# Summing eight expert rows per token: halves of the eight rows, or halves of the row

## The chip, the cores and the metric

One Trainium2 chip, one core of it. The metric is the device time of one execution in microseconds (us); less is better. All times of lines and windows come from one profiled execution, counted from the start of its span.

## The reference, cut to what matters

The program is a small diffusion backbone: two layers over 256 latent tokens (and, in layer 0, 256 context tokens beside them), width 1024. Each layer is a token mixer followed by a mixture of experts in which each token goes to 8 of 64 experts. What the change touches is the last step of a layer: for each token the eight rows that its experts wrote are summed, the sum is scaled by the gate `g2` and added to the residual stream, and the stream is normalised for what comes next (the first norm of layer 1, or the final norm).

```python
def rms_norm(x, g):
    y = xf * lax.rsqrt(jnp.mean(xf * xf, axis=-1, keepdims=True) + RMS_EPS)
    return (y * g.astype(jnp.float32)).astype(x.dtype)
...
        routed = jnp.zeros((T + 1, D), f32).at[tok_buf].add(y.reshape(P, D))[:T]
...
        h = modulate(rms_norm(x, norm1_g[i]), sh1, sc1)
...
        x = x + g2 * f[:B * S].reshape(B, S, D)
    return rms_norm(x, final_g)
```

All of it is fp32. The expert rows are already multiplied by their routing weights, and the shared expert was added to the stream earlier, so the step here is a plain sum of eight rows.

## The kernel before

The kernel is one program of phases, each a block in which all five engines have their own instruction list and which ends with all of them meeting. Within a phase the engines are ordered by semaphores only; nothing of the next phase starts before the last one is over. The phase that the change touches is `combine_phase` (L1747 on), which runs twice: in layer 0 over 4 tiles of 128 tokens, in layer 1 over 2 tiles. In the second run it is also the end of the program.

The experts have scattered their rows to the DRAM tensor `y_rows`, so that the eight rows of a token (TOPK = 8, 1024 floats, 4 KB each) lie one behind the other. A tile is 128 tokens on 128 partitions, and its 4 MB are loaded in two parts of 2 MB into four buffers of `c_rows`. Part 0 is the first four rows of each token, part 1 the last four; on either side a partition's piece is 16 KB in one run.

* SyncE (L1778 to L1781) issues the loads in order, tile by tile, part 0 then part 1; after the first two it issues the loads of the next modulation rows (two of 1 MB, layer 0) or of the final gain (0.5 MB, layer 1). A load of tile t from t = 2 on waits until the tile two before is out of its buffer: part 0 on TensorE (`pe_summed`), part 1 on VectorE (`summed`).
* TensorE (L1795 to L1803) sums part 0: four rows times two halves of 512 columns, each a matmul with the identity that accumulates in PSUM.
* VectorE (L1813 to L1829) sums part 1 with an add over 2048 elements a partition (L1816) and one over 1024 (L1818), then adds TensorE's sum from PSUM (L1821), multiplies by the gate (L1823) and adds to the stream `x_stream` (L1825), 1024 elements a partition each.
* ScalarE (L1807 to L1809) takes the row's sum of squares (L325) and the root (L327) when the stream's tile is complete.
* VectorE finishes the norm (L332, L334 and, in layer 0 alone, L340). It does so one tile late: after tile t's adds it does the norm of tile t-1, and the last tile's norm follows behind the loop.

In layer 1 the two tiles of `h` are then stored to the output (L1789).

Of the kernel before, what the change touches and what calls it, by code (L numbers as in the profile page):

```python
# [25 lines left out]
ALU = mybir.AluOpType  # L26
ACT = mybir.ActivationFunctionType
AX = mybir.AxisListType

P = 128  # L30
D = 1024
# [31 lines left out]
TOPK = 8  # L63
# [1683 lines left out]
def combine_phase(g, layer, tiles):  # L1747


    nc = g.nc  # L1750
    tag = f"c{layer}"
    H = D // 2
    KH = TOPK // 2
    jobs = [(t, part) for t in range(tiles) for part in range(2)]
    with ExitStack() as st:
        sb = lambda n, s, d=F32: st.enter_context(nc.sbuf_tensor(f"{tag}_{n}", s, d))
        rows = sb("rows", [P, 4, KH, D])
        total = sb("total", [P, 2, D])
        rows_in = [g.sem(f"{tag}_rows_in{q}") for q in range(4)]
        summed, pe_summed, scaled = g.sem(f"{tag}_summed"), g.sem(f"{tag}_pe_summed"), g.sem(f"{tag}_scaled")  # L1760
        halved, merged = g.sem(f"{tag}_halved"), g.sem(f"{tag}_merged")
        src = g.y_rows[0:tiles * P * TOPK, :].rearrange("(t p k) d -> t p k d", p=P, k=TOPK)
        added, mod_in, stored = g.sem(f"{tag}_added"), g.sem(f"{tag}_mod_in"), g.sem(f"{tag}_stored")
        gate2 = [g.mod(t, GATE2) for t in range(tiles)]
        if layer == 0:
            g.mod_layer = 1
            norm = NormRows(g, "n3", lambda t: g.mod(t, SH1), lambda t: g.mod(t, SC1))
        else:
            gain = sb("gain", [P, D])
            norm = NormRows(g, "nf", None, lambda t: gain[:])  # L1770
        with nc.Block() as block:
            @block.sync
            def _(sp):
                def load_mods():
                    for dst, stream, a, b in MOD_LOADS1[0:2]:
                        sp.dma_start(g.mod_slots(dst, b - a), g.mod_source(1, stream, a, b)).then_inc(mod_in, 16)

                for n, (t, part) in enumerate(jobs):  # L1778
                    if n >= 4:
                        sp.wait_ge(pe_summed if part == 0 else summed, t - 1)  # L1780
                    sp.dma_start(rows[:, n % 4, :, :], src[t][:, part * KH:(part + 1) * KH, :]).then_inc(rows_in[n % 4], 16)  # L1781
                    if n == 1 and layer == 0:
                        load_mods()
                    if n == 1 and layer == 1:
                        sp.dma_start(gain[:], g.ins["final_g"].partition_broadcast(P)).then_inc(mod_in, 16)  # L1785
                if layer == 1:
                    for t in range(tiles):
                        sp.wait_ge(norm.ready, t + 1)
                        sp.dma_start(g.out[0, t * P:(t + 1) * P, :], g.h[:, t, :]).then_inc(stored, 16)  # L1789
                    sp.wait_ge(stored, 16 * tiles)  # L1790

            @block.tensor
            def _(pe):

                for t in range(tiles):  # L1795
                    pe.wait_ge(rows_in[2 * (t % 2)], 16 * (t // 2 + 1))
                    if t >= 2:
                        pe.wait_ge(merged, t - 1)
                    for k in range(KH):
                        for n in range(2):  # L1800
                            last = pe.matmul(g.ps[:, 2 * (t % 2) + n, :], g.ident, rows[:, 2 * (t % 2), k, n * H:(n + 1) * H],  # L1801
                                             start=(k == 0), stop=(k == KH - 1))
                    last.then_inc(pe_summed, 1)  # L1803

            @block.scalar
            def _(act):
                for t in range(tiles):  # L1807
                    act.wait_ge(added, t + 1)
                    norm.act(act, t)  # L1809

            @block.vector
            def _(dve):
                for t in range(tiles):  # L1813
                    b, sums = 2 * (t % 2) + 1, total[:, t % 2, :]
                    dve.wait_ge(rows_in[b], 16 * (t // 2 + 1))
                    dve.tensor_tensor(rows[:, b, 0:2, :], rows[:, b, 0:2, :], rows[:, b, 2:4, :], ALU.add).then_inc(halved, 1)  # L1816
                    dve.wait_ge(halved, t + 1)
                    dve.tensor_tensor(sums, rows[:, b, 0, :], rows[:, b, 1, :], ALU.add).then_inc(summed, 1)  # L1818
                    dve.wait_ge(summed, t + 1)
                    dve.wait_ge(pe_summed, t + 1)  # L1820
                    dve.tensor_tensor(sums, g.ps[:, 2 * (t % 2):2 * (t % 2) + 2, :].rearrange("p a b -> p (a b)"), sums, ALU.add).then_inc(merged, 1)  # L1821
                    dve.wait_ge(merged, t + 1)
                    dve.tensor_tensor(sums, sums, gate2[t], ALU.mult).then_inc(scaled, 1)  # L1823
                    dve.wait_ge(scaled, t + 1)
                    dve.tensor_tensor(g.x[:, t, :], g.x[:, t, :], sums, ALU.add).then_inc(added, 1)  # L1825
                    if t:
                        dve.wait_ge(mod_in, 32 if layer == 0 else 16)
                        norm.dve(dve, t - 1)
                norm.dve(dve, tiles - 1)  # L1829


# [401 lines left out]
def backbone(nc, ins, table, out):  # L2233
    with ExitStack() as stack:
# [16 lines left out]
        with ExitStack() as layer:  # L2251
            g.mods_rest = layer.enter_context(nc.sbuf_tensor("mods_rest", [P, 4, D], F32))
            ada_phase(g)
            turned = ExitStack()
            with ExitStack() as att:
                sb = lambda n, s, d=F32: att.enter_context(nc.sbuf_tensor(n, s, d))
                qT = sb("qT", [P, HEADS // 2, TOK])
                kT = sb("kT", [P, KV // 2, 2, TOK])
                v = sb("v", [P, TILES, KVD])
                qkv_phase(g, qT, kT, v)  # L2260
                o = sb("o", [P, TILES, QD])
                attention_phase(g, qT, kT, v, o)
                g.turned_rows(turned, "hT0", TILES)
                project_phase(g, "ao", ins["attn_w_o"][0].rearrange("(p k) n -> p k n", k=KD), P, KD, TILES, src=o, spare=(qT, kT, v))
            with ExitStack() as moe:
                sb = lambda n, s, d=F32: moe.enter_context(nc.sbuf_tensor(n, s, d))
                routes, weights = Routes(sb, 0, TILES), ExpertWeights(g, sb, 0)
                route_phase(g, 0, TILES, routes, weights)
                turned.close()
                expert_phase(g, 0, TILES, routes, weights)  # L2270
            combine_phase(g, 0, TILES)
        g.recycle_semaphores()

        with ExitStack() as layer:
            turned = ExitStack()
            with ExitStack() as lru:
                sb = lambda n, s, d=F32: lru.enter_context(nc.sbuf_tensor(n, s, d))
                hsum = sb("hsum", [RP, RB, SEQ])
                with ExitStack() as inner:
                    sb = lambda n, s, d=F32: inner.enter_context(nc.sbuf_tensor(n, s, d))  # L2280
                    par = sb("par", [RW, 11 * RB])
                    uc = sb("uc", [RP, RB, TOK])
                    gate = sb("gate", [P, LAT_TILES, RNN])
                    lru_in_phase(g, par, uc, gate, hsum)
                    lru_scan_phase(g, par, uc, gate, hsum)
                g.turned_rows(turned, "hT1", LAT_TILES)
                project_phase(g, "lo", ins["lru_w_out"][0].rearrange("(n c) d -> c n d", c=RW), RW, RB, LAT_TILES, srcT=hsum)
            with ExitStack() as moe:
                sb = lambda n, s, d=F32: moe.enter_context(nc.sbuf_tensor(n, s, d))
                routes, weights = Routes(sb, 1, LAT_TILES), PairWeights(g, sb, 1)  # L2290
                route_phase(g, 1, LAT_TILES, routes, weights)
                turned.close()
                expert_pair_phase(g, 1, LAT_TILES, routes, weights)
            combine_phase(g, 1, LAT_TILES)
# [70 lines left out]
```

## Time and profile before

| what | value |
|---|---|
| median of 3 runs | 2297.92 us (2296.35 to 2297.92) |
| the profiled execution's own time | 2296.35 us |
| its span, first to last instruction | 2294.5 us |
| busy: TensorE matmul, VectorE, ScalarE | 83%, 49%, 34% of the span |
| the combine phase of layer 0 | from 1203.1 to 1263.1 us |
| the combine phase of layer 1 | from 2257.4 to the span's end |
| the two together | some 97 us, 4% of the span |

The profile's shares are averages over phases with different limits, and for this change they say little: the busiest engine of the whole, TensorE, is not what sets the length of the combine phase. That has to be read from the timeline of the two stretches, engine by engine.

### The profile page before, as it was taken

What the parts mean: (1) busy time and instruction counts of PE and PEld (TensorE: products, weight loads), DVE (VectorE), ACT (ScalarE), POOL (GpSimd) and SP (SyncE); (2) the same over time, 40 slices, a digit from 0 to 9 for tenths busy, and PEclk for the clock granted to TensorE, in tenths of its full rate; (3) what the DMA queues carried; (4) which work ended last, traced back from release to release, by engine and by line L of the source; (5) the groups of instructions that cost most, each with busy time, mean ns of one, the idle gap of its engine ahead of it and who ended that gap; (6) DMA issues with size and microseconds to landing.
All of it is one profiled execution on the core that took longest, in us unless ns stands there. A gap on an engine that the chain in (4) does not pass through costs nothing. (4 is left out here: it accounts for less than half of the span.)

```text
span 2294.5 us, 33559 instructions
## 1 busy us (share of the span) xinstructions
PE 1910.6 (83%) x9971; PEld 1297.1 (57%) x9972; DVE 1132.9 (49%) x2243; ACT 791.6 (34%) x1283; POOL 318.2 (14%) x333
## 2 busy tenths in 40 slices
PE   2889997889999999999986886637778788888884
PEld 0778844467777777777762881103445455555552
DVE  2325622577777777777756555893132121121123
ACT  1214411145555555555531456870101111111111
POOL 0220010011111111121110102221001111111110
PEclk9999997989999999999997997768889999999997
DMA  6850054158998899999957416304439999999994
GB/s 242 288 201 2 1 227 166 45 211 322 345 340 328 331 333 347 346 340 336 339 179 325 132 54 199 118 17 129 187 136 420 412 383 404 399 414 392 412 408 199
DMA packets 128294, 597.07 MB, mean 260 GB/s; under 512 B 32633, under 2 KB 51129, under 8 KB 67441
## 3 DMA queue, kind: packets, MB, share of 16 engines
q1 hardware_dynamic: 92512, 509.97, 58.5%
q0 software_dynamic: 35584, 84.31, 9.8%
q10 hardware_dynamic: 144, 2.10, 0.2%
q8 instruction: 31, 0.51, 0.1%
q14 instruction: 23, 0.18, 0.0%
HBM read 596.17 MB, written 56.20 MB: 284 GB/s over the span
## 5 line engine op out<-in xcount | busy, mean ns | idle before, releaser
L1459 DVE TENSOR_TENSOR m_w_lo<-m_wgu,m_w_hi 128x1024 fp32r<-128x1024 f32 x264 | 314.9, 1222 | 159.9 <-ACT m_w_hi L1383 145.8
L1383 ACT ACTIVATE m_w_hi<-m_wgu 128x1024 fp32r<-128x1024 f32 x264 | 269.7, 1053 | 196.0 <-DMA m_wgu<-in_moe_w_up 133.1
L1630 PE MATMUL ps<-m_wgu,m_xT 128*64 128x256 f32 x2112 | 262.2, 404 | 75.5 <-DMA m_wgu<-in_moe_w_up 58.6
L1630 PEld LDWEIGHTS ps<-m_wgu,m_xT 128*64 128x64 f32 x2112 | 186.3, 146 | 162.5 <-issue 118.8
L1325 PE MATMUL ps<-m_wd,m_hidT 128*128 128x512 f32 x528 | 237.6, 593 | 0.3 <-ACT m_hidT L1407 0.3
L1340 PE MATMUL ps<-m_w_hi,m_x_hi 128*128 128x512 f32 x528 | 213.2, 404 | 6.7 <-DVE m_x_lo L1451 6.3
L1340 PE MATMUL ps<-m_w_lo,m_x_hi 128*128 128x512 f32 x528 | 208.5, 395 | 0.0
L1340 PE MATMUL ps<-m_w_hi,m_x_lo 128*128 128x512 f32 x528 | 207.8, 394 | 0.0
L1725 DVE SCALAR_TENSOR_TENSOR m_hid<-m_act_g,m_meta,ps 128x256 f32<-128x256 f32 x33 | 15.9, 481 | 335.3 <-ACT m_act_g L1679 335.3
L1325 PEld LDWEIGHTS ps<-m_wd,m_hidT 128*128 128x128 f32 x528 | 95.3, 190 | 95.1 <-issue 95.1
L1266 POOL DMA_INDIRECT y_rows<-h,m_sidx x66 | 67.6, 1024 | 554.4 <-DVE h L1467 554.4
L1657 PE MATMUL ps<-m_wd,m_hidT 128*64 128x512 f32 x528 | 123.8, 610 | 21.9 <-ACT m_hidT L1682 14.7
L1679 ACT ACTIVATE m_act_g<-ps 128x256 f32<-128x256 f32 x33 | 12.7, 384 | 313.0 <-PE ps L1630 313.0
L1340 PEld LDWEIGHTS ps<-m_w_hi,m_x_hi 128*128 128x128 f32 x528 | 100.5, 190 | 26.5 <-issue 7.1
L1340 PEld LDWEIGHTS ps<-m_w_lo,m_x_hi 128*128 128x128 f32 x528 | 100.3, 190 | 21.5
L1340 PEld LDWEIGHTS ps<-m_w_hi,m_x_lo 128*128 128x128 f32 x528 | 100.5, 190 | 19.2
L325 ACT ACTIVATE squares<-x_stream 128x1024 bf16<-128x1024 f32 x16 | 16.9, 1053 | 261.8 <-DVE x_stream L864 140.7
L1657 PEld LDWEIGHTS ps<-m_wd,m_hidT 128*64 128x64 f32 x528 | 42.5, 139 | 80.5 <-issue 80.5
L1575 POOL DMA_INDIRECT h<-h_rows,m_gidx x35 | 35.6, 1017 | 376.4 <-DVE m_gidx L1713 370.2
L1451 DVE TENSOR_TENSOR m_x_lo<-ps,m_x_hi 128x512 fp32r<-128x512 f32 x134 | 85.9, 683 | 0.5 <-ACT m_x_hi L1373 0.5
L1801 PE MATMUL ps<-c_rows,table 128*128 128x512 f32 x96 | 51.5, 698 | 41.4 <-DMA c_rows<-y_rows 41.4
L1390 ACT ACTIVATE h<-ps 128x512 f32<-128x512 f32 x66 | 39.4, 597 | 130.2 <-PE ps L1325 130.2
(317 smaller groups left out, 3438.5 us busy)
## 6 DMA issues: line engine op xcount, KB each, us to landing
m_wgu<-in_moe_w_gate SPq DMA_DIRECT2D x132, 1024.0 KB
m_wgu<-in_moe_w_up SPq DMA_DIRECT2D x132, 1024.0 KB
m_wd<-in_moe_w_down SPq DMA_DIRECT2D x132, 1024.0 KB, 9.7
c_rows<-y_rows SPq DMA_DIRECT2D x12, 2048.0 KB, 14.9
mods<-in_ada_w POOLq DMA_DIRECT2D x11, 1024.0 KB, 6.6
mods<-in_ada_w SPq DMA_DIRECT2D x11, 1024.0 KB, 4.9
mods<-in_lru_w_in SPq DMA_DIRECT2D x7, 1280.0 KB, 6.9
ada_w<-in_ada_w SPq DMA_DIRECT2D x8, 1024.0 KB, 17.8
```

Source lines behind the costliest of these rows:

```text
L325: act.activation(g.junk[:], g.x[:, t, :], ACT.Square, accum_out=g.sumsq[:, t:t + 1]).then_inc(self.squared, 1)
L1266: pool.indirect_dma_start(g.y_rows[0:tiles * P * TOPK, :], bass.IndirectOffsetOnAxis(ap=sidx[q][:, 0:1], axis=0), ysb[q], None, bounds_che ...
L1325: last = pe.matmul(g.ps[0:S, YB + n, :], hidT[:, j, :], wd[:, q, j, n * 512:(n + 1) * 512], start=(j == 0), stop=(j == KF - 1))
L1340: last = pe.matmul(g.ps[0:S, GU, :].rearrange("p (a f) -> p a f", a=2), x[:, q, k, :], w[:, :, k, :], start=(k == 0 and n == 0), stop=(k = ...
L1383: act.activation(w_hi[:, :, k, :], wgu[:, q, :, k, :], ACT.Copy).then_inc(hi_s, 1)
L1390: act.activation(ysb[q][:, 0:512], g.ps[0:S, YB, :], ACT.Copy).then_inc(y_a, 1)
L1451: dve.tensor_tensor(x_lo[:, q, ks, :], g.ps[:, XB + n, 0:4 * S].rearrange("p (k c) -> p k c", c=S), x_hi[:, q, ks, :].bitcast(F32), ALU.su ...
L1459: dve.tensor_tensor(w_lo[:, :, k, :], wgu[:, q, :, k, :], w_hi[:, :, k, :].bitcast(F32), ALU.subtract).then_inc(lo_s, 1)
L1575: pool.indirect_dma_start(xg, None, g.h2_rows[0:tiles * P, :], bass.IndirectOffsetOnAxis(ap=gidx[:, 0:1], axis=0), bounds_check=last_token ...
L1630: last = pe.matmul(g.ps[half[s], GU, a * FE:(a + 1) * FE], xT[:, k, half[s]], wgu[:, s, a, k, :], start=(k == 0), stop=(k == KD - 1))
L1657: last = pe.matmul(g.ps[half[s], YB + n, :], hidT[:, j, half[s]], wd[:, s, j, n * 512:(n + 1) * 512], start=(j == 0), stop=(j == KF - 1))
L1801: last = pe.matmul(g.ps[:, 2 * (t % 2) + n, :], g.ident, rows[:, 2 * (t % 2), k, n * H:(n + 1) * H], start=(k == 0), stop=(k == KH - 1))
```

## The change

The two parts of a tile are cut the other way. Part h is now half h of the columns (512 of 1024) of all eight rows, so a partition's 16 KB come as eight pieces of 2 KB, 4 KB apart in DRAM. TensorE sums the eight rows of the left half (h = 0) in one PSUM bank, VectorE those of the right half (h = 1), with one `tensor_reduce` over the eight rows in place of two adds. The reduce reads `rows` as "p d k", so its innermost step is from one row to the next, 512 floats or 2 KB apart. The two halves need no merging: the gate multiply and the add to the stream are done per half, on 512 elements, first for h = 1, then for h = 0, whose multiply reads PSUM. The norm of tile t now follows at once behind tile t's adds instead of one tile later. The semaphores `halved` and `merged` go.

```diff
-    KH = TOPK // 2
-    jobs = [(t, part) for t in range(tiles) for part in range(2)]
+    jobs = [(t, h) for t in range(tiles) for h in range(2)]
...
-        rows = sb("rows", [P, 4, KH, D])
-        total = sb("total", [P, 2, D])
+        rows = sb("rows", [P, 4, TOPK, H])
+        total = sb("total", [P, 2, H])
...
-                    sp.dma_start(rows[:, n % 4, :, :], src[t][:, part * KH:(part + 1) * KH, :]).then_inc(rows_in[n % 4], 16)
+                    sp.dma_start(rows[:, n % 4, :, :], src[t][:, :, h * H:(h + 1) * H]).then_inc(rows_in[n % 4], 16)
...
-                        pe.wait_ge(merged, t - 1)
-                    for k in range(KH):
-                        for n in range(2):
-                            last = pe.matmul(g.ps[:, 2 * (t % 2) + n, :], g.ident, rows[:, 2 * (t % 2), k, n * H:(n + 1) * H],
-                                             start=(k == 0), stop=(k == KH - 1))
+                        pe.wait_ge(scaled, 2 * (t - 1))
+                    for k in range(TOPK):
+                        last = pe.matmul(g.ps[:, t % 2, :], g.ident, rows[:, 2 * (t % 2), k, :], start=(k == 0), stop=(k == TOPK - 1))
...
-                    act.wait_ge(added, t + 1)
+                    act.wait_ge(added, 2 * (t + 1))
...
-                for t in range(tiles):
-                    b, sums = 2 * (t % 2) + 1, total[:, t % 2, :]
-                    dve.wait_ge(rows_in[b], 16 * (t // 2 + 1))
-                    dve.tensor_tensor(rows[:, b, 0:2, :], rows[:, b, 0:2, :], rows[:, b, 2:4, :], ALU.add).then_inc(halved, 1)
-                    dve.wait_ge(halved, t + 1)
-                    dve.tensor_tensor(sums, rows[:, b, 0, :], rows[:, b, 1, :], ALU.add).then_inc(summed, 1)
-                    dve.wait_ge(summed, t + 1)
-                    dve.wait_ge(pe_summed, t + 1)
-                    dve.tensor_tensor(sums, g.ps[:, 2 * (t % 2):2 * (t % 2) + 2, :].rearrange("p a b -> p (a b)"), sums, ALU.add).then_inc(merged, 1)
-                    dve.wait_ge(merged, t + 1)
-                    dve.tensor_tensor(sums, sums, gate2[t], ALU.mult).then_inc(scaled, 1)
-                    dve.wait_ge(scaled, t + 1)
-                    dve.tensor_tensor(g.x[:, t, :], g.x[:, t, :], sums, ALU.add).then_inc(added, 1)
-                    if t:
+                for n, (t, h) in enumerate((t, h) for t in range(tiles) for h in (1, 0)):
+                    q = n % 2
+                    x = g.x[:, t, h * H:(h + 1) * H]
+                    gate = gate2[t][:, h * H:(h + 1) * H]
+                    if h == 0:
+                        dve.wait_ge(pe_summed, t + 1)
+                        sums = g.ps[:, t % 2, :]
+                    else:
+                        b = 2 * (t % 2) + 1
+                        dve.wait_ge(rows_in[b], 16 * (t // 2 + 1))
+                        sums = total[:, q, :]
+                        dve.tensor_reduce(sums, rows[:, b, :, :].rearrange("p k d -> p d k"), AX.X, ALU.add).then_inc(summed, 1)
+                        dve.wait_ge(summed, t + 1)
+                    dve.tensor_tensor(total[:, q, :], sums, gate, ALU.mult).then_inc(scaled, 1)
+                    dve.wait_ge(scaled, n + 1)
+                    dve.tensor_tensor(x, x, total[:, q, :], ALU.add).then_inc(added, 1)
+                    if h == 0 and t + 1 < tiles:
+
                         dve.wait_ge(mod_in, 32 if layer == 0 else 16)
-                        norm.dve(dve, t - 1)
+                        norm.dve(dve, t)
                 norm.dve(dve, tiles - 1)
```

## Rows read from the trace of the kernel before

**Rows 1.** The timeline, layer 0: start us, us, engine, line, operation, tiles [idle before, releaser].

```profile
1203.10 0.81 SPq L1781 DMA_DIRECT2D c_rows<-y_rows  x2
...
1215.19 2.29 DVE L1816 TENSOR_TENSOR c_rows<-c_rows 128x2048 f32<-128x2048 f32 x1 [17.65 <-DMA c_rows<-y_rows]
...
1222.55 1.23 DVE L1825 TENSOR_TENSOR x_stream<-x_stream,c_total 128x1024 f32<-128x1024 f32 x1
...
1229.94 2.29 DVE L1816 TENSOR_TENSOR c_rows<-c_rows 128x2048 f32<-128x2048 f32 x1 [6.16 <-DMA c_rows<-y_rows]
...
1240.55 2.29 DVE L1816 TENSOR_TENSOR c_rows<-c_rows 128x2048 f32<-128x2048 f32 x1
...
1244.63 8.83 PE L1801 MATMUL ps<-c_rows,table 128*128 128x512 f32 x16 [2.65 <-DMA c_rows<-y_rows]
...
1250.44 2.28 DVE L1816 TENSOR_TENSOR c_rows<-c_rows 128x2048 f32<-128x2048 f32 x1
...
1260.33 0.16 DVE L332 RECIPROCAL rstd<-root 128x1 f32<-128x1 f32 x1
...
1261.84 1.22 DVE L340 TENSOR_TENSOR h<-h,mods 128x1024 f32<-128x1024 f32 x1
```

**Rows 2.** The timeline, layer 1, same columns.

```profile
2269.68 2.29 DVE L1816 TENSOR_TENSOR c_rows<-c_rows 128x2048 f32<-128x2048 f32 x1 [21.81 <-DMA c_rows<-y_rows]
...
2279.57 1.28 ACT L327 ACT_TABLE_LOAD   x1
...
2281.13 2.29 DVE L1816 TENSOR_TENSOR c_rows<-c_rows 128x2048 f32<-128x2048 f32 x1 [2.76 <-DMA c_rows<-y_rows]
...
2287.23 1.23 DVE L1825 TENSOR_TENSOR x_stream<-x_stream,c_total 128x1024 f32<-128x1024 f32 x1
...
2290.00 0.16 DVE L332 RECIPROCAL rstd<-root 128x1 f32<-128x1 f32 x1
2290.20 1.28 DVE L334 SCALAR_TENSOR_TENSOR h<-x_stream,rstd,c_gain 128x1024 f32<-128x1024 f32 x1
```

**Rows 3.** Groups by line and form, VectorE, whole span: | busy us, mean ns | idle before.

```profile
L1818 DVE TENSOR_TENSOR c_total<-c_rows 128x1024 f32<-128x1024 f32 x6 | 7.3, 1224 | 0.2
...
L221 DVE TENSOR_TENSOR h<-ps,h 128x512 f32<-128x512 f32 x2 | 1.4, 691 | 16.0 <-PE ps L214 16.0
```

**Rows 4.** The same view: reduces and short operations of VectorE.

```profile
L677 DVE TENSOR_REDUCE top<-ps 128x1 f32<-128x512 f32 x32 | 21.9, 685 | 4.3 <-PE ps L610 4.3
...
L677 DVE TENSOR_REDUCE top<-ps 128x1 f32<-128x256 f32 x32 | 13.3, 417 | 2.2 <-PE ps L610 2.2
...
L1121 DVE TENSOR_SCALAR r_chosen<-r_chosen 128x256 f32<-128x256 f32 x1 | 0.3, 293 | 0.0
...
L1121 DVE TENSOR_SCALAR r_chosen<-r_chosen 128x128 f32<-128x128 f32 x1 | 0.2, 226 | 0.0
...
L1099 DVE TENSOR_TENSOR r_gscore<-r_best 128x32 f32<-128x32 f32 x1 | 0.2, 216 | 0.0
...
L2175 DVE TENSOR_TENSOR ls_dd<-ls_dd,ls_m 80x32 f32<-80x32 f32 x1 | 0.2, 187 | 0.0
...
L1099 DVE TENSOR_TENSOR r_gscore<-r_best 128x16 f32<-128x16 f32 x1 | 0.2, 186 | 0.0
```

**Rows 5.** DMA of the window 1205 to 1250 us, combine phase, layer 0.

```profile
DMA packets 1424, 18.61 MB, mean 414 GB/s; under 512 B 160, under 2 KB 160, under 8 KB 160
...
q1 hardware_dynamic: 1424, 18.61, 97.1%
```

**Rows 6.** DMA of the window 1268 to 1275 us, loads in pieces of 1280 B.

```profile
q1 hardware_dynamic: 1636, 2.02, 82.8%
```

**Rows 7.** DMA of the window 60 to 72 us, loads in pieces of 512 B.

```profile
q1 hardware_dynamic: 6109, 3.03, 91.1%
```

More of the change, by code:

```diff
@@ L1752, in combine_phase @@
     H = D // 2
-    KH = TOPK // 2
-    jobs = [(t, part) for t in range(tiles) for part in range(2)]
+    jobs = [(t, h) for t in range(tiles) for h in range(2)]
     with ExitStack() as st:
         sb = lambda n, s, d=F32: st.enter_context(nc.sbuf_tensor(f"{tag}_{n}", s, d))
-        rows = sb("rows", [P, 4, KH, D])
-        total = sb("total", [P, 2, D])
+        rows = sb("rows", [P, 4, TOPK, H])
+        total = sb("total", [P, 2, H])
         rows_in = [g.sem(f"{tag}_rows_in{q}") for q in range(4)]
         summed, pe_summed, scaled = g.sem(f"{tag}_summed"), g.sem(f"{tag}_pe_summed"), g.sem(f"{tag}_scaled")
-        halved, merged = g.sem(f"{tag}_halved"), g.sem(f"{tag}_merged")
         src = g.y_rows[0:tiles * P * TOPK, :].rearrange("(t p k) d -> t p k d", p=P, k=TOPK)
@@ L1776, in load_mods @@
                         sp.dma_start(g.mod_slots(dst, b - a), g.mod_source(1, stream, a, b)).then_inc(mod_in, 16)
-                for n, (t, part) in enumerate(jobs):
+                for n, (t, h) in enumerate(jobs):
                     if n >= 4:
-                        sp.wait_ge(pe_summed if part == 0 else summed, t - 1)
-                    sp.dma_start(rows[:, n % 4, :, :], src[t][:, part * KH:(part + 1) * KH, :]).then_inc(rows_in[n % 4], 16)
+                        sp.wait_ge(pe_summed if h == 0 else summed, t - 1)
+                    sp.dma_start(rows[:, n % 4, :, :], src[t][:, :, h * H:(h + 1) * H]).then_inc(rows_in[n % 4], 16)
                     if n == 1 and layer == 0:
```

## The prediction

> **What bounds the kernel now.** The page's busy shares come first, and they are a warning: TensorE is busiest over the whole, but the change lies in two stretches of some 97 us together, where other things decide. So the next view is the timeline of each stretch, read along VectorE, because every tile ends there.
>
> In layer 0 [rows 1] VectorE's first add of a tile (L1816) starts at 1215.19, 1229.94, 1240.55 and 1250.44. The first two have a DMA as releaser, after 17.65 and 6.16 us of idleness: rows are late. The other two have no wait shown. Loads come at about 4.9 us per 2 MB, as 1215.19 to 1229.94 holds three pairs' worth of megabytes (4 MB of rows, 2 MB of modulation rows: 14.75 / 3 = 4.92 us per 2 MB), so a tile of 4 MB takes 9.8 us; VectorE's own work on a tile, 1240.55 to 1250.44, is 9.9 us. The phase is balanced: DMA leads for two tiles, VectorE for the rest. The reader should see here that any lengthening of VectorE's tile is paid in full. The last rows land about 1249.5, one load (4.9 us) behind the 1244.63 at which TensorE was released by the last part 0; the norm of the last tile ends at 1263.06.
>
> In layer 1 [rows 2] both tiles wait for DMA (2269.68, 2281.13). From 2281.13 to the last instruction's end at 2291.48 it is a chain: five VectorE operations, 1.54 us of ScalarE (2288.46 to 2290.00), the norm's last two operations. The output store and the program's end follow.
>
> **The change part by part.** The unit prices first. A half-width operation: 0.69 us (the 128x512 row), 0.72 from start to start; the full-width one is 1.224 [rows 3]. ScalarE's squares and root, seen from VectorE: 1.54 us, and 1.28 more for a phase's first tile, because of the table load [rows 2]. The norm itself: 1260.33 to 1263.06 = 2.73 us in layer 0 [rows 1], 2290.00 to 2291.48 = 1.48 in layer 1 [rows 2].
>
> *TensorE.* Eight matmul calls of 512 columns a tile before and after; nothing gained or lost. The left half's sum needs the first-landed part alone, 8.83 us or less behind it, and VectorE asks for it only after the reduce and two half-width operations. Hidden.
>
> *VectorE's adds.* Removed: 2.29 + 4 x 1.224 and gaps = 7.3 us a tile. Added: one reduce over 4096 elements a partition, of length R, and four half-width operations, 2.88 us.
>
> *R* is the whole question, and no row shows it: no reduce of the trace is this long or reads 2 KB steps. Bounds: two reduces over contiguous data give (685 - 417) / 256 = 1.047 ns an element and 149 ns fixed [rows 4], so R = 0.15 + 4.29 = 4.44 us if the step costs nothing. One kind of VectorE operation reads in large steps: L1099 takes elements 32 B apart. With 32 elements it lasts 216 ns where the contiguous one lasts 187, 0.91 ns more an element; and from 16 to 32 elements it grows by 30 ns, 1.88 ns an element [rows 4]. That gives 4096 x (1.047 + 0.91) + 150 = 8.2 us, or 0.15 + 4096 x 1.875 ns = 7.8 us. I take 8.1. The row is short, and it reads two such operands where the reduce reads one, so the lower bound keeps a real chance; but it is the nearest row, and it shows the element rate nearly halved.
>
> The Trainium skill (SBUF — State Buffer, Specifications) says that SBUF has lines of 16 bytes, that full bandwidth needs at least two hits on a line, and that each crossing to a new line pays a penalty. It gives no price. A step of 2 KB hits each line once, so this rule speaks against the reduce as written; L1099 agrees with it.
>
> *The order of the norm.* Before, the norm of tile t-1 ran after tile t's adds, so ScalarE's 1.54 us lay beside other work except for the last tile, and there too the previous norm filled it. Now VectorE stands still 1.54 us for every tile (2.82 for the first of a phase), with the next tile's reduce queued behind it. In layer 0 a tile costs VectorE R + 2.88 + 1.54 + 2.73 = R + 7.15, in layer 1 R + 5.90.
>
> *The buffers.* SyncE's loads of tiles 2 and 3, right halves, wait for the reduce (`summed`). With R = 8.1 tile 0's reduce ends near 1224.5, when three loads are still queued, and tile 1's near 1241, so that the last load lands near 1249, 14 us before it is wanted. Nothing is late from this.
>
> *The loads.* 128 pieces of 16 KB a load become 1024 of 2 KB. A packet's time on an engine (share x 16 engines x window / packets): 491 ns for 13.1 KB on average in this phase, which the 160 small ones pull down; without them about 553 ns for 14.7 KB, 26.6 B/ns [rows 5]. Pieces of 1280 B: 56.7 ns for 1235 B [rows 6], where 26.6 B/ns would take 46.4, so 10 ns more a packet; pieces of 512 B: 28.6 ns for 496 B [rows 7] against 18.6, again 10 ns. A load has 64 packets an engine now instead of 8, so 56 x 10.4 ns = 0.6 us more, 5.5 instead of 4.9. Bounds: nothing, or 1280 B's rate in full (1235 / 56.7 x 16 = 348 GB/s, 6.0 us, 1.1 more). The start of each phase shows it twice: 1.2 us. After that the loads stay hidden behind VectorE in the forecast.
>
> *Sum, layer 0.* Start 1215.2 + 1.2 = 1216.4; tile 1 starts 8.1 + 7.15 + 1.28 later, 1232.9 (its rows land at 1229.94 + 4 x 0.6 = 1232.3, in time); then three tiles of 15.25: 1278.7. Before 1263.06: **+15.6**.
> *Layer 1.* Start 2269.7 + 1.2 = 2270.9; tile 0 ends 8.1 + 5.90 + 1.28 later, 2286.2 (last rows land 2283.5); tile 1 ends 14.0 later, 2300.2. Before 2291.48: **+8.7**. The store of tile 0 leaves earlier, that of tile 1 leaves behind the last norm as before.
>
> Sum: +24.3 us, against the profiled execution's own 2296.35: 2320.7. The median of the runs is 1.57 us above it, within their own spread; I say **2321 us**.
>
> **The rivals.** 0.2% (4.6 us) is about what a measurement of this kernel can tell from no change.
>
> *The step costs nothing (B).* R = 4.44. Then VectorE's tile is 11.6 us and loads take 11.0 a tile. With the loads 0.6 slower: tile 1 starts at 1232.3, three tiles end at 1267.1, +4.0; layer 1: 2283.5 + 4.44 + 5.90 = 2293.8, +2.4. In all +6.4, 2303. With unchanged loads: 1229.94 + 34.8 = 1264.7, +1.6, and +0.2 in layer 1 (tile 0 ends at 2269.7 + 4.44 + 7.18 = 2281.3, + 10.3): +1.8, 2298. With loads at the 1280 B rate, 1.1 us more each, the last landings are 8.8 and 4.4 us later: 1258.3 + 11.6 and 2285.5 + 10.3 give +6.8 and +4.3, 2307. For it: L1099 may pay only because it fetches two streams. Against: L1099 itself.
>
> *Faster (D).* The reduce takes two elements per beat, as the contiguous tensor_scalar rows do ((293 - 226) / 128 = 0.52 ns an element [rows 4]): R = 2.3. Place: the last tile's chain behind the last landing. With unchanged loads layer 0 ends at 1249.5 + 2.3 + 7.15 = 1259.0, -4.1, and layer 1 at 2281.1 + 8.2 = 2289.3, -2.2: -6.3, 2290. From the formulas with unchanged loads (3R - 11.7 in layer 0, R - 4.5 in layer 1) it decides below R = 4.0, and clears 4.6 us only below R = 2.9. Against: the contiguous reduces run at 1.05 ns, and slower loads take nearly all of the gain. The Trainium skill (VectorE: DVE Perf Modes, The perf-mode tier table) has tensor_reduce at one element a cycle in every case; the L677 rows agree.
>
> *The loads halve (C).* If eight pieces 4 KB apart cost half the rate, 9.8 us per 2 MB: landing of the last in layer 0 at 1203.1 + 2.3 + 8 x 9.8 + 4.9 = 1288.7, end at + 15.25 = 1304, +41; in layer 1 (2257.5 + 2.4 + 4 x 9.8 + 1.2 = 2300.3, + 14.0) +22.8; in all +64, 2360. DMA takes over from VectorE only above 7.6 us per load. Against: pieces smaller than these run at 348 GB/s [rows 6].
>
> **How the numbers follow.** Forecast (A, R between 7.5 and 9, loads 0 to 1.1 slower): 0.60. B: 0.28. C, or a step still dearer than two beats: 0.07. D: 0.03. The rest, 0.02, spread. A's own range: below 8.1, R = 7.5 with unchanged loads is six tiles x 0.6 less and 2.4 less, 2314.7; R = 9 with the dear loads is 5.4 and 2 more, 2328; so 2314 to 2329. For 8 in 10 B's middle must be in: 2300 to 2331. Slower by over 0.2%: all of A and C, and B above +4.6, about 0.20 of its 0.28: 0.87. Within: the rest of B and D with slower loads, 0.10. Faster: 0.03.
>
> **What would show it.** The reduce's mean, near 8.1 us, six times. Four idle gaps of about 1.5 us (2.8 for the first) ahead of the reciprocal (L332) in layer 0, released by ScalarE's root. Starts of the reduces in layer 0 near 1216.4, 1232.9, 1248.2, 1263.4, counted as in this trace, with no DMA wait ahead of the last two. Load packets of 2 KB near 87 ns. TensorE long idle between tiles. The prediction is wrong if the reduce is at 4.4 us, when DMA waits stand ahead of each tile; and if the loads fall under 275 GB/s (2.1 MB in 7.6 us).

## The result, and the profile after

The changed kernel takes 2318.98 us (median of 5 runs, 2310.95 to 2324.4) against 2297.92; the ratio is 1.0089, 95% interval 1.0074 to 1.0104. That is 21 us or 0.9% slower. The forecast was 2321. The profiled execution took 2321.31 us, its span 2319.5.

The timeline of the changed kernel in layer 0, VectorE alone: start us, us, engine, line, operation [idle before, releaser].

```profile
1218.75 7.11 DVE L1820 TENSOR_REDUCE c_total<-c_rows 128x512 f32<-128x4096 f32 x1 [20.61 <-DMA c_rows<-y_rows]
...
1231.53 0.17 DVE L332 RECIPROCAL rstd<-root 128x1 f32<-128x1 f32 x1 [2.90 <-ACT root L327]
...
1234.65 7.15 DVE L1820 TENSOR_REDUCE c_total<-c_rows 128x512 f32<-128x4096 f32 x1 [0.38 <-DMA c_rows<-y_rows]
...
1246.20 0.16 DVE L332 RECIPROCAL rstd<-root 128x1 f32<-128x1 f32 x1 [1.61 <-ACT root L327]
...
1248.86 7.10 DVE L1820 TENSOR_REDUCE c_total<-c_rows 128x512 f32<-128x4096 f32 x1
...
1263.01 7.03 DVE L1820 TENSOR_REDUCE c_total<-c_rows 128x512 f32<-128x4096 f32 x1
...
1274.36 0.16 DVE L332 RECIPROCAL rstd<-root 128x1 f32<-128x1 f32 x1 [1.54 <-ACT root L327]
1274.56 1.28 DVE L334 SCALAR_TENSOR_TENSOR h<-x_stream,rstd,mods 128x1024 f32<-128x1024 f32 x1
1275.88 1.23 DVE L340 TENSOR_TENSOR h<-h,mods 128x1024 f32<-128x1024 f32 x1
```

The chain that ended last, in order of time, from the first load of layer 1 (start us, us, what):

```profile
2273.99 0.56 SPq L1779
...
2274.60 14.78 DMA c_rows<-y_rows
...
2289.40 7.09 DVE c_total L1820
...
2303.64 6.99 DVE c_total L1820
...
2313.43 1.16 ACT squares L325 x2
...
2315.14 1.28 DVE h L334
```

Set beside [rows 1, 2], three things can be seen. Where before two of four tiles of layer 0 waited for rows, now VectorE works or waits for ScalarE from 1218.75 on, but for 0.38 us: it is the bound. The reduce is 7.0 to 7.15 us long in all six tiles. And each tile has a hole ahead of the reciprocal, released by ScalarE's root, as forecast.

From here on the measure is the length of a combine phase, from the issue of its first load to the end of the norm's last operation; it leaves out what the rest of the program does in one execution and not in another. Before: 1203.10 to 1263.06 and 2257.46 to 2291.48. After: 1203.70 to 1277.11 and 2273.99 to 2316.42.

| kernel | layer 0 | layer 1 | both | against before |
|---|---|---|---|---|
| before | 59.96 | 34.02 | 93.98 | |
| changed | 73.41 | 42.43 | 115.84 | +21.86 |
| e1: other steps in the reduce | 71.83 | 42.48 | 114.31 | +20.3 |
| e2: adds for the reduce | 65.35 | 37.40 | 102.75 | +8.8 |
| e3: before, with a reduce | 70.49 | 37.70 | 108.19 | +14.2 |
| e4: before, norm at once | 62.54 | 35.08 | 97.62 | +3.6 |
| e5: changed, norm late | 70.95 | 40.67 | 111.62 | +17.6 |
| e6: changed, adds, norm late | 65.43 | 37.44 | 102.87 | +8.9 |
| e7: before, 4 KB pieces | 61.58 | 36.04 | 97.62 | +3.6 |
| e8: columns split, 16 KB pieces | 57.98 | 32.73 | 90.71 | -3.3 |
| e9: second load on another queue | 77.43 | 43.55 | 120.98 | +27.0 |
| e10: larger pieces first | 77.17 | 42.78 | 119.95 | +26.0 |
| e11: other steps in an add | 69.87 | 39.43 | 109.30 | +15.3 |

The rest of the span, which is the same code in all of them, was 2200.5 us before, 2203.7 after, from 2197.5 to 2205.9 in e1 to e10, and 2221.0 in e11, which passes other sums on to layer 1. So 3 us of the difference between the two profiled executions, and up to 8 us between any two of the others, say nothing of the combine phases. In e7 this hides the loss altogether: its phases are 3.6 us longer than before, and its one timed execution took 2296.87 us.

How steady the phases are can be seen where kernels share a stretch: from the first issue to VectorE's first sum of layer 0 it is 12.1 to 12.5 us in before, e3 and e4, and 15.0 to 15.5 us in changed, e1, e2, e5, e6 and e11. Each phase was traced once per kernel, so differences of under 1 us between two phases are not read here.

The loads. DMA of the changed kernel in the window 1220 to 1245 us:

```profile
GB/s 419 442 416 347 393 390 383 383 393 387 393 383 383 393 383 390 383 383 396 380 387 390 383 393 380 387 393 380 390 387 383 400 377 387 390 380 390 387 390 390
DMA packets 4509, 9.73 MB, mean 389 GB/s; under 512 B 85, under 2 KB 85, under 8 KB 4400
...
q1 hardware_dynamic: 4509, 9.73, 104.3%
```

A packet of 2158 B on average takes 1.043 x 16 x 25 us / 4509 = 92.5 ns. That window still holds some hundred packets of 8 KB, of the modulation rows. The window 1230 to 1245 us holds none:

```profile
q1 hardware_dynamic: 2882, 5.80, 105.0%
```

There a packet takes 1.05 x 16 x 15 us / 2882 = 87.4 ns, and 87 were forecast. TensorE's starts on tiles 1 to 3 lie 10.8 us apart against 9.8 before, 5.4 us per load against 4.9.

### The profile page after: what moved, and what is told of

It reads as the page before. It is cut to its first block and busy times, and to the rows that moved or that the text cites. A ratio compares the mean times of both kernels' runs of the same rounds, so it can differ in the third digit from the quotient of the medians.

```text
span 2319.5 us, 33553 instructions
## 1 busy us (share of the span) xinstructions
PE 1913.9 (83%) x9971; PEld 1296.5 (56%) x9972; DVE 1148.0 (49%) x2243; ACT 792.0 (34%) x1283; POOL 317.4 (14%) x333
## 5 line engine op out<-in xcount | busy, mean ns | idle before, releaser
L1433 DVE TENSOR_SCALAR m_onehot<-table,l_slot 128x128 f32<-128x128 f32 x280 | 78.1, 344 | 13.0 <-PE ps L1301 6.5
```

The costliest lines, as they stand in the source:

```text
L1433: last = dve.tensor_scalar(onehot[:, q, t, :], g.field("iota")[:, 0:S], routes.slot[:, t, bass.ds(e, 1)], g.table[:, bass.ds(b + FIELD[f"n ...
```

## The experiments

### The reduce

**e1: the step alone.** The view that the reduce reads is cut otherwise in each tile:

```diff
-dve.tensor_reduce(sums, rows[:, b, :, :].rearrange("p k d -> p d k"), AX.X, ALU.add)
+step = ((1, 2, 4, 8) if layer == 0 else (64, 512))[t]
+dve.tensor_reduce(sums.rearrange("p (a s) -> p a s", s=step),
+                  rows[:, b, :, :].rearrange("p k d -> p (k d)").rearrange("p (a k s) -> p a s k", k=TOPK, s=step), AX.X, ALU.add)
```

> The changed kernel, its reduce reading a different step between the eight summed elements in each tile: 4, 8, 16 and 32 bytes in the four tiles of layer 0, 256 bytes and 2 KB in the two of layer 1. It sums other elements than the reference, so only its times count. Each reduce still takes 4096 elements a partition to 512. Theory (the step is what costs): 4.4 us at 4 and 8 bytes, 7.1 at 256 bytes and 2 KB, the turn at 16 or 32 bytes. Rival (a reduce with many outputs costs 1.7 ns an element at any step): 7.1 us in all six. Second rival (the cost grows with the step, as a matter of rows or banks): 256 bytes well under 2 KB.

Its timeline; the steps are 4, 8, 16, 32 bytes, then 256 bytes and 2 KB:

```profile
1221.22 4.42 DVE L1821 TENSOR_REDUCE c_total<-c_rows 128x512 f32<-128x4096 f32 x1 [21.06 <-DMA c_rows<-y_rows]
...
1237.09 4.42 DVE L1821 TENSOR_REDUCE c_total<-c_rows 128x512 f32<-128x4096 f32 x1 [3.02 <-DMA c_rows<-y_rows]
...
1248.56 7.41 DVE L1821 TENSOR_REDUCE c_total<-c_rows 128x512 f32<-128x4096 f32 x1
...
1263.02 7.46 DVE L1821 TENSOR_REDUCE c_total<-c_rows 128x512 f32<-128x4096 f32 x1
...
2290.11 7.10 DVE L1821 TENSOR_REDUCE c_total<-c_rows 128x512 f32<-128x4096 f32 x1 [25.07 <-DMA c_rows<-y_rows]
...
2304.29 7.07 DVE L1821 TENSOR_REDUCE c_total<-c_rows 128x512 f32<-128x4096 f32 x1
```

One instruction, the same elements, only the step differs. At 4 and 8 bytes it is 4.42 us, which is the 4.44 worked out from the contiguous reduces of [rows 4]; from 16 bytes on it is 7.1 to 7.5, and growing the step to 2 KB adds nothing. The place in the phase is not the cause: at a step of 2 KB the same four tiles of layer 0 took 7.03 to 7.15 us. Both rivals fall. The Trainium skill (SBUF — State Buffer, Specifications) asks for at least two hits on a line of 16 bytes for full bandwidth; two fp32 elements share one at a step of 8 bytes and none do at 16, which is exactly where the turn is. The price measured here is 1.7 to 1.8 ns an element instead of 1.05.

**e11: the same on a plain add.** The sum is now three adds, and the first of them (2048 elements a partition) reads and writes with other steps in each tile:

```diff
+turn = lambda a: a.rearrange("p k d -> p d k")
+flat = lambda a: a.rearrange("p k d -> p (k d)").rearrange("p (d k) -> p d k", k=4)
+near = lambda a, s: a.rearrange("p k d -> p (k d)").rearrange("p (a k s) -> p a s k", k=4, s=s)
+ops = ((turn(out), turn(lo), turn(hi)), (flat(out), turn(lo), turn(hi)), (flat(out), flat(lo), turn(hi)), (turn(out), flat(lo), flat(hi)),
+       (near(out, 2), near(lo, 2), near(hi, 2)), (near(out, 4), near(lo, 4), near(hi, 4)))[t if layer == 0 else 4 + t]
+dve.tensor_tensor(*ops, ALU.add)
```

> The changed kernel with adds, the first of them (2048 elements, two inputs) with other steps in each tile and its own output buffer: layer 0 tile 0 both inputs and the output in 2 KB steps; tile 1 both inputs in 2 KB steps, output contiguous; tile 2 one input in 2 KB steps; tile 3 only the output in 2 KB steps; layer 1 tile 0 everything in 8 byte steps; tile 1 everything in 16 byte steps. It sums other elements than the reference in four of the six tiles, so only its times count. Contiguous the add took 2.29 us. Theory (a read that meets another 16 bytes with every element costs near 1.7 to 1.9 ns an element in any operation): 3.6 to 3.9 us with both inputs or one in steps and at 16 bytes, 2.29 with the output alone and at 8 bytes. Rival (each slow stream pays for itself): one input 3.0, both 3.7. Rival (only reduces pay; the short row of before misled): 2.29 in all.

Its timeline, the six adds in the order of the expectation:

```profile
1219.95 3.85 DVE L1828 TENSOR_TENSOR c_four<-c_rows 128x2048 f32<-128x2048 f32 x1 [20.77 <-DMA c_rows<-y_rows]
...
1235.79 3.93 DVE L1828 TENSOR_TENSOR c_four<-c_rows 128x2048 f32<-128x2048 f32 x1 [1.58 <-DMA c_rows<-y_rows]
...
1248.76 3.67 DVE L1828 TENSOR_TENSOR c_four<-c_rows 128x2048 f32<-128x2048 f32 x1
...
1261.89 3.67 DVE L1828 TENSOR_TENSOR c_four<-c_rows 128x2048 f32<-128x2048 f32 x1
...
2303.17 2.29 DVE L1828 TENSOR_TENSOR c_four<-c_rows 128x2048 f32<-128x2048 f32 x1 [25.05 <-DMA c_rows<-y_rows]
...
2315.64 3.88 DVE L1828 TENSOR_TENSOR c_four<-c_rows 128x2048 f32<-128x2048 f32 x1 [1.03 <-DMA c_rows<-y_rows]
```

One stepped input costs nearly as much as two and an output (3.67 against 3.85), so most of the price is paid once an instruction, and it is paid for a stepped output alone too, which I had expected to be free. A second stepped input adds 0.26 us (3.93). The short row L1099 of [rows 4] was thus no accident of its two streams. It gave 1.88 ns an element; here, less 0.16 us that do not grow with the elements (from the contiguous adds of 2.29 us and 1.224), two stepped inputs cost 1.84 ns and one costs 1.71.

**e2: adds in place of the reduce**, in the changed kernel:

```diff
-dve.tensor_reduce(sums, rows[:, b, :, :].rearrange("p k d -> p d k"), AX.X, ALU.add).then_inc(summed, 1)
+dve.tensor_tensor(rows[:, b, 0:4, :], rows[:, b, 0:4, :], rows[:, b, 4:8, :], ALU.add).then_inc(halved, 1)
+dve.wait_ge(halved, 2 * t + 1)
+dve.tensor_tensor(rows[:, b, 0:2, :], rows[:, b, 0:2, :], rows[:, b, 2:4, :], ALU.add).then_inc(halved, 1)
+dve.wait_ge(halved, 2 * t + 2)
+dve.tensor_tensor(sums, rows[:, b, 0, :], rows[:, b, 1, :], ALU.add).then_inc(summed, 1)
```

> The changed kernel with the reduce replaced by three adds of halves (2048, 1024 and 512 elements), all contiguous, 4.26 us with gaps; loads and norm order as changed. The two combine phases, from the first load's issue to the norm's last operation, were 59.96 and 34.02 us before (93.98) and 73.41 and 42.43 after (115.84). Theory (the reduce's step carries most of it, the slower loads the rest): layer 0 about 64.9, layer 1 about 38.0, together 103, so 13 of the 22 us come back and 9 stay. Rival (the norm's new place carries it): under 5 us come back. Rival (the loads are slow only because buffers are released late): nothing stays, 94 to 96.

Measured 65.35 and 37.40, 102.75 in all: 13.1 us come back, 8.8 stay. The three adds, in its timeline, with the wait that takes the reduce's place:

```profile
1237.88 2.29 DVE L1821 TENSOR_TENSOR c_rows<-c_rows 128x2048 f32<-128x2048 f32 x1 [3.28 <-DMA c_rows<-y_rows]
1240.21 1.23 DVE L1823 TENSOR_TENSOR c_rows<-c_rows 128x1024 f32<-128x1024 f32 x1
1241.47 0.69 DVE L1825 TENSOR_TENSOR c_total<-c_rows 128x512 f32<-128x512 f32 x1
...
1260.95 2.29 DVE L1821 TENSOR_TENSOR c_rows<-c_rows 128x2048 f32<-128x2048 f32 x1
```

From the first add's start to the third's end it is 4.28 us. The last line shown, tile 3, has no wait for rows.

**e3: a reduce alone, in the kernel before**, for its two adds:

```diff
-dve.tensor_tensor(rows[:, b, 0:2, :], rows[:, b, 0:2, :], rows[:, b, 2:4, :], ALU.add).then_inc(halved, 1)
-dve.wait_ge(halved, t + 1)
-dve.tensor_tensor(sums, rows[:, b, 0, :], rows[:, b, 1, :], ALU.add).then_inc(summed, 1)
+dve.tensor_reduce(sums, rows[:, b, :, :].rearrange("p k d -> p d k"), AX.X, ALU.add).then_inc(summed, 1)
```

> The kernel before with only its two adds replaced by one reduce over the four rows: 4096 elements to 1024, step 4 KB, loads in 16 KB pieces and the norm late. Theory: the reduce lasts about 7.1 us, layer 0 about 70.4 us (59.96 before), layer 1 about 37.6 (34.02), in all +14. Rival (the reduce was slow because it reads what the 2 KB loads wrote, or beside their packets): 4.4 us and no more than +3 in all. If the time goes by outputs, not inputs, the reduce with twice the outputs is dearer than 7.1.

Measured 70.49 and 37.70, +14.2 in all, with reduces of 7.08 to 7.21 us:

```profile
1217.76 7.18 DVE L1816 TENSOR_REDUCE c_total<-c_rows 128x1024 f32<-128x4096 f32 x1 [18.08 <-DMA c_rows<-y_rows]
```

Twice the outputs make no difference, nor do the pieces that the loads come in.

### The place of the norm

**e4: the norm at once, in the kernel before.**

```diff
-                    if t:
+                    if t + 1 < tiles:
                         dve.wait_ge(mod_in, 32 if layer == 0 else 16)
-                        norm.dve(dve, t - 1)
+                        norm.dve(dve, t)
```

> The kernel before with only the norm moved to its own tile, as the change does. Theory (hidden behind the loads nearly everywhere while the sums are short): VectorE's tile in layer 0 11.6 us instead of 9.9, the phase 61.6 instead of 59.96, layer 1 34.2 instead of 34.02; +1.8 in all. Rival (each tile pays ScalarE's 1.54 and the first the table load): 4 x 1.54 + 1.28 and 2 x 1.54 + 1.28, +12 in all.

Measured +3.6, twice what I expected. Its timeline shows the part that I had left out:

```profile
1231.72 2.29 DVE L1816 TENSOR_TENSOR c_rows<-c_rows 128x2048 f32<-128x2048 f32 x1 [0.40 <-DMA c_rows<-y_rows]
1234.05 1.23 DVE L1818 TENSOR_TENSOR c_total<-c_rows 128x1024 f32<-128x1024 f32 x1
1236.14 1.22 DVE L1821 TENSOR_TENSOR c_total<-ps,c_total 128x1024 f32<-128x1024 f32 x1 [0.87 <-PE ps L1801]
```

VectorE waits 0.87 us for TensorE's sum in tile 1 of layer 0, and 0.68 us in the first tile of layer 1, and both times it then has no wait for rows: it is the bound and pays them, 1.55 of the 1.8 us by which I was short. The wait is not new. In the kernel before it was 1.39 us in the first tile of layer 1, but there it lay in slack, with 2.76 us of waiting for rows behind it; in tile 1 of layer 0 it was 0.74 us, with no wait for rows behind it either, and the expectation had counted without it. In the changed kernel TensorE's half is wanted last and this wait does not occur.

**e5: the norm late again, in the changed kernel** (the same edit the other way round, for h = 0).

> The changed kernel with only the norm put back to one tile late. Theory: VectorE's tile in layer 0 12.7 us instead of 14.15, layer 0 about 71.7 (73.41 changed), layer 1 about 41.0 (42.43); 3.2 us less in all. Rival (the place of the norm costs nothing): no difference. Rival (it costs its whole wait every time): 6 x 1.54 = 9 less.

Measured 70.95 and 40.67, 4.2 us less than changed. From its timeline:

```profile
1248.59 7.06 DVE L1820 TENSOR_REDUCE c_total<-c_rows 128x512 f32<-128x4096 f32 x1
...
1258.35 0.15 DVE L332 RECIPROCAL rstd<-root 128x1 f32<-128x1 f32 x1
...
1261.00 7.04 DVE L1820 TENSOR_REDUCE c_total<-c_rows 128x512 f32<-128x4096 f32 x1
```

The holes in layer 0 are gone: its reciprocals have no wait, and the reduces follow each other in 12.4 us instead of 14.15.

**e6: adds, and the norm late.** Only the cut of the sums by columns and its loads are left.

> The changed kernel with adds in place of the reduce and the norm late: what is left of the change is the cut by columns, with its 2 KB loads. Theory (the loads alone): first reduce's place 15 us behind the first issue instead of 12.1, then 10.9 us a tile; layer 0 about 65.2, layer 1 about 38.1, in all +9 against before. Rival (the loads keep up once VectorE is quick): within 2 us of before. The norm's place should make no difference of more than 1 us here against the kernel with adds and the norm at once, since the loads lead.

Measured 102.87, +8.9 against before, and 0.1 from e2. Its last tile of layer 0:

```profile
1257.83 2.29 DVE L1821 TENSOR_TENSOR c_rows<-c_rows 128x2048 f32<-128x2048 f32 x1 [0.98 <-DMA c_rows<-y_rows]
```

With these loads and short sums the place of the norm makes no difference to the whole. In layer 1 VectorE waits for rows of tile 1 either way (0.59 us in e2, 4.95 here). In layer 0 it is a draw of another kind. In e2 VectorE has no wait for rows from tile 2 on, its tiles lie 11.3 and 11.7 us apart where two loads take 10.8, and its last sum starts 54.0 us behind the first issue, here 53.1; but behind that start e2 has 11.3 us of work and this kernel 12.4, because the norm of tile 2 comes there too. With the long reduce the norm's place costs 4.2 us.

What a part costs depends on what it is added to: the reduce 14.2 us in the kernel before (e3), 13.1 in the changed one (e2), 8.75 with the changed loads and the norm late (e5 - e6); the norm's place 3.6 (e4), nothing (e2 against e6) and 4.2 (changed - e5). Taken in one order they are loads and cut +8.9, reduce +8.75, norm +4.2; that these give 21.9 is arithmetic and tests nothing.

### The loads

**e7: pieces of 4 KB, in the kernel before.** Part 0 is the even rows, part 1 the odd ones:

```diff
-sp.dma_start(rows[:, n % 4, :, :], src[t][:, part * KH:(part + 1) * KH, :])
+sp.dma_start(rows[:, n % 4, :, :], src[t][:, part::2, :])
```

> The kernel before with only its parts cut another way: even and odd rows of the eight, so a load is 512 pieces of 4 KB instead of 128 of 16 KB (1024 of 2 KB in the change). In the change the first load took 9.3 us from issue to TensorE's start instead of 7.2, later ones 5.43 instead of 4.9. Theory (a cost for every piece, at the start too): first load 8.1 us, later ones 5.15; layer 0 +2 to +3.5, layer 1 +1 to +2. Rival (only pieces under 4 KB pay): 7.2, 4.9 and no change.

TensorE's starts on tiles 1 and 2 in its timeline:

```profile
1225.36 8.89 PE L1801 MATMUL ps<-c_rows,table 128*128 128x512 f32 x16 [5.55 <-DMA c_rows<-y_rows]
...
1235.60 7.13 PE L1801 MATMUL ps<-c_rows,table 128*128 128x512 f32 x16 [1.35 <-DMA c_rows<-y_rows]
```

Measured: first load 7.9 us from issue to TensorE's start, the tiles' starts 10.24 us apart (5.12 per load), layer 0 +1.6 (a little under what was expected), layer 1 +2.0. So every further piece costs, those of 4 KB too: 24 more packets an engine for 0.22 us, 9 ns each; from 8 to 64 packets it is 5.43 - 4.90 = 0.53 us, 9.5 ns each. The forecast had 10.

**e9: the second load on another queue.** Left open was the start. The first pair ended 15.05 and 15.41 us behind the first issue, 12.09 and 12.22 before. Two loads at the later rate explain 1.1 of these 3 us.

```diff
             def _(act):
+                act.dma_start(rows[:, 1, :, :], src[0][:, :, H:D]).then_inc(rows_in[1], 16)
```

> The changed kernel with the second load of each phase (right half of tile 0) issued from ScalarE's queue instead of SyncE's; everything else as changed. Open is why the first pair of loads ends 15.05 and 15.41 us behind its issue, when two loads at the later rate (5.4 us) and the start that the kernel before shows (2.3 us) give 13.1. In the slices of the first microseconds the engines were busy and moved some 290 GB/s. Theory (the queue is slow to supply small pieces at first, so a second queue helps): the pair ends at 13 to 13.8 us. Rival (small pieces are slow at the start of a phase whoever issues them): 15, as changed.

In layer 0 the pair ended 19.49 us behind the first issue, in layer 1 16.47, and the phases are 4.0 and 1.1 us longer than in the changed kernel. But this does not test the start alone: the loads behind the pair, 2 MB of modulation rows and 0.5 MB of gain, now ran beside it. What was moved in the first 20 us from the first issue of layer 0 can be compared, first the changed kernel, then this one:

```profile
DMA packets 2655, 6.88 MB, mean 344 GB/s; under 512 B 64, under 2 KB 64, under 8 KB 2399
...
DMA packets 2733, 7.04 MB, mean 352 GB/s; under 512 B 64, under 2 KB 64, under 8 KB 2477
```

That is 0.16 MB more with the second queue (0.25 MB in layer 1), worth 0.4 and 0.6 us at the later 387 GB/s. So the slow start got a little shorter, not the 1 to 2 us of the theory, and as the pair shares the engines with what was behind it, the kernel loses by it.

**e10: the larger pieces first.**

```diff
+                if layer == 0:
+                    load_mods()
+                else:
+                    sp.dma_start(gain[:], g.ins["final_g"].partition_broadcast(P)).then_inc(mod_in, 16)
                 for n, (t, h) in enumerate(jobs):
```

> The changed kernel with the modulation rows (2 MB in 8 KB pieces) issued ahead of the first rows in layer 0, and the gain (0.5 MB) in layer 1, instead of behind the first pair. In layer 0 the pair then lands behind 2 MB more. Theory (the queue supplies pieces slowly at first; while the 8 KB pieces move it gets ahead): start 2.3 + 4.9 + two loads of 5.4 = 18.0 us for the pair's end in layer 0, and its rate is 385 GB/s from the first. Rival (the first small pieces are slow whatever runs ahead): 20 us.

DMA of this kernel, in slices of 0.5 us from its first issue (1204.50):

```profile
GB/s 0 66 197 197 426 393 442 360 426 328 459 475 344 320 377 352 279 283 389 397 389 393 414 401 406 393 336 299 315 393 401 401 401 385 410 389 389 381 389 393
```

The pair ended 19.3 us behind the first issue (1204.50 to 1223.80), between the two expectations. The rate falls to 280 to 380 GB/s where the small pieces begin, behind the 2 MB of large ones, and recovers; it falls once more, to 300 to 340, some 4 us after that. The slow spell goes with the first small pieces, not with the phase's beginning, and it was shortened by about 0.6 us (15.05 and 4.9 for the 2 MB ahead would be 19.95). In layer 1, where 0.5 MB ran ahead, the pair ended at 15.72, some 0.9 us less than the same sum gives (15.41 + 1.2). Both phases are longer than in the changed kernel, so this is no remedy either. Why the engines need longer for these packets than for the later ones of the same size was not settled.

### A version that beats both

**e8.** The loads stay as before, in 16 KB pieces by rows; only the sums are cut by columns. Each engine takes its half of the columns of each part as it lands. So there are no two sums of the same columns to merge, and behind the last landing VectorE has less left to do.

```diff
+                for t in range(tiles):
+                    for part in range(2):
+                        b = 2 * (t % 2) + part
+                        pe.wait_ge(rows_in[b], 16 * (t // 2 + 1))
...
+                        for k in range(KH):
+                            last = pe.matmul(g.ps[:, t % 2, :], g.ident, rows[:, b, k, 0:H],
+                                             start=(part == 0 and k == 0), stop=(part == 1 and k == KH - 1))
+                        last.then_inc(pe_summed, 1)
...
+                    for part in range(2):
+                        dve.wait_ge(rows_in[b + part], 16 * (t // 2 + 1))
+                        dve.tensor_tensor(half[:, part, :, :], rows[:, b + part, 0:2, H:D], rows[:, b + part, 2:4, H:D], ALU.add).then_inc(summed, 1)
+                    dve.wait_ge(summed, 2 * t + 2)
+                    dve.tensor_tensor(half[:, 0, :, :], half[:, 0, :, :], half[:, 1, :, :], ALU.add).then_inc(halved, 1)
+                    dve.wait_ge(halved, 2 * t + 1)
+                    dve.tensor_tensor(total[:, 0, 0:H], half[:, 0, 0, :], half[:, 0, 1, :], ALU.add).then_inc(halved, 1)
```

The gate and the add to the stream follow per half as in the change; the norm is late as before; a buffer's next load waits for both engines.

> A version that may beat both: loads in 16 KB pieces as before, but TensorE sums the left half of the columns of all eight rows and VectorE the right half with adds, four rows as soon as each part lands; no merging operation, norm one tile late. VectorE's chain behind the last landing is 6.1 us instead of 7.3. Theory: layer 0 about 58.5 us (59.96), layer 1 about 32.8 (34.02), 2.6 us less in all, 0.1%, at the edge of what the time can tell. Rival (buffers now wait for both engines, so loads come later and eat it): no less than before. Rival (TensorE's part behind the last landing at the low clock is the longer one): layer 1 above 34.

Measured 57.98 and 32.73, 3.3 us less than before. Timed: 2296.63 us median of 11 runs beside 2299.63 of 15, ratio 0.9981, interval 0.9971 to 0.9990: 0.2% faster, small but clear of 1. The last tile of layer 1 in its timeline:

```profile
2277.51 1.23 DVE L1820 TENSOR_TENSOR c_half<-c_rows 128x1024 f32<-128x1024 f32 x1 [3.45 <-DMA c_rows<-y_rows]
2277.53 3.70 PE L1804 MATMUL ps<-c_rows,table 128*128 128x512 f32 x8 [1.17 <-DMA c_rows<-y_rows]
2278.77 1.23 DVE L1822 TENSOR_TENSOR c_half<-c_half 128x1024 f32<-128x1024 f32 x1
...
2282.81 0.69 DVE L1833 TENSOR_TENSOR x_stream<-x_stream,c_total 128x512 f32<-128x512 f32 x1
```

From the landing to the stream's last add it is 2277.51 to 2283.50, 6.0 us, where [rows 2] have 2281.13 to 2288.46, 7.3. TensorE's 3.70 us are over at 2281.2, ahead of the 2282.09 at which VectorE reads them.

## Why the prediction was right

**The reduce** (8.1 us forecast, 7.1 measured). The argument held: the only row with large steps, L1099, forecast that a 2 KB step slows the reduce, and e1 and e11 show that it is the step and nothing else. The size came out 1.0 us high. e11 tells where some of it lies: at its 1.84 ns for two stepped inputs 4096 elements would take 7.7 us, at its 1.71 ns for one 7.2 (estimates, with the reduce's 0.15 us). So about half a microsecond is the second stream of L1099, which the prediction named as a doubt and did not price; the rest, from 7.7 to the 8.1 taken, comes of an excess of 29 or 30 ns read from a row of 16 and 32 elements. Six tiles at 1.0 less are 6 us of the sum.

**The norm's place** was charged as worked out: holes of 1.54 to 1.61 us and 2.90 for the first, per-tile work of R + 7.05 in layer 0 (14.15) against R + 7.15. What the prediction did not say is how much of the loss hangs on it: 4.2 us here, 3.6 in the kernel before (e4), and nothing where the loads lead (e2, e6).

**The loads.** 5.5 us each forecast, 5.43 measured; 87 ns a packet forecast, 87.4 measured. The first pair was mis-sized: +1.2 us forecast, +3.0 and +3.2 measured. The 3.8 us too little in the two phases made up for most of the reduce's 6 too much, and that is luck: the forecast starts of the four reduces of layer 0, 1216.4, 1232.9, 1248.2 and 1263.4, were 1218.75, 1234.65, 1248.86 and 1263.01.

**The buffers** were no trouble, as said: no reduce from tile 2 on waits for DMA. But the working is off. It lands the last load of layer 0 near 1249, as in the kernel before, where its own 0.6 us more for each of eight loads gives 1254.3. DMA of the changed kernel in slices of 0.3 us from 1250:

```profile
GB/s 369 396 375 396 382 389 389 382 389 382 403 362 362 314 307 212 102 82 41 0 0 0 0 0 0 0 0 0 0 0 0 0 0 0 0 0 0 0 27 0
```

The last rows are in at about 1255.7, 7 us ahead of the reduce at 1263.01 and not 14. **TensorE** was hidden.

**The sum**: +15.6 and +8.7 forecast, +13.45 and +8.4 measured, 24.3 against 21.9. The two profiled executions differ by 24.96 us, nearer still to 24.3, but 3 us of that lie in code that is the same in both, so this nearness is luck. The forecast of 2321 also leaves out the 1.57 us by which the median before lay above its profiled execution; with them it would be 2322.2, against 2318.98 measured.

**The rivals.** B, a step that costs nothing, is what e2 comes close to (sums of 4.28 us, +8.8; B was put at +6.4, without the slow start). D and C did not occur: the reduce took 4.42 us over contiguous data (e1), not 2.3, and a load took 11% longer, not twice as long.

## What to carry to other kernels

Before an operation is turned so that one instruction replaces several, look at the innermost step of every operand in bytes: on fp32, 8 bytes were free and 16 or more cost 60 to 70% more, so three contiguous adds (4.28 us) beat one stepped reduce (7.1) over the same data. Cut the sum by columns and leave the loads in long runs: the two cuts need not be the same (e8). And a wait moved into the loop is free only as long as that engine is not the bound.

## What the runs showed of the hardware that was not expected

* A stepped output alone costs VectorE's add as much as stepped inputs: 3.67 us for either, against 2.29 contiguous (e11, e2). Two stepped inputs cost 3.93.
* Steps of 16 and 32 bytes were somewhat dearer for the reduce than 256 bytes and 2 KB: 7.41 and 7.46 us against 7.10 and 7.07 (e1).
* Each packet of a load cost 9 to 9.5 ns beyond its bytes, at 4 KB as at 2 KB (e7, changed).
* The first small pieces of a phase run slower than later ones of the same size: 1.9 and 2.1 us in the two phases beyond the packets' price. Behind larger pieces it was 0.6 and 0.9 us less (e10), with a second queue 0.4 and 0.6 us (e9). The cause is open.
